# Triangular doubling in the recurrent stage: 32 of 64 columns per product, packed in PSUM, copied back with a stride

## The chip, the core and the metric

The kernel runs on one core of a Trainium2 chip. The metric is the device time of one execution in microseconds; the kernel before takes 2091.57 us (median of 3 runs, 2091.12 to 2100.21).

## What is computed

Two transformer blocks on one sequence of 512 tokens and width 1024. The change is in the second block, in its RWKV-7 branch (8 heads of 64, two directions). The reference computes it token by token:

```python
def step(state, inp):
    r_t, w_t, k_t, v_t, a_t, b_t = inp
    sa = jnp.einsum('dbhij,dbhj->dbhi', state, a_t)
    state = (state * w_t[..., None, :] + sa[..., :, None] * b_t[..., None, :]
             + v_t[..., :, None] * k_t[..., None, :])
    y = jnp.einsum('dbhij,dbhj->dbhi', state, r_t)
    return state, y
```

The kernel computes it in chunks of 64 tokens. Inside a chunk it needs the inverse of a triangular 64x64 matrix (identity minus the masked product of a and b). It gets it by doubling: the inverses of the 1x1 diagonal blocks give those of the 2x2 blocks, these those of the 4x4 blocks, and so on in six levels.

## The kernel before

`rwkv_block` holds the whole branch. Its engines run written-out programs in order, with semaphores between them, inside one block; the next stage (`merge_block`) starts its first weight load only when all engines have left it.

The work is cut into 8 units, `u`: four pairs of heads (`fi`) times two directions (`d = u % 2`). For one unit TensorE does in this order: `attention(u)`, the products of the scaled r, k, a, b (`r_bank<-r_b_s,r_a_s` and the like); the doubling levels `double(u, k)` for k = 1 to 5; between level 1 and 2 the products `keys_values(u)` and the two `lora_products` of the next unit; after level 5 `late(u)`: the product of the inverse with `wr`, the transposes of the next unit's tiles (`turn`), and the products that make the chunk's output and state. Level 0 is done on VectorE with masks (L2307).

At a level the tiles are `ab_t` (the masked matrix), `x` and `x_t` (the inverse so far and its transpose) and `z`. Each is 128 partitions by 2 heads (`hh`) by 4 token tiles (`NB`) by 64 columns; the lower and the upper 64 partitions are two chunks (`half`). A call of `block_products` (L2021) is one group: 8 matmuls of 64x64 weights, 4 tiles times 2 halves, each half on its own quadrant of the array. A matmul in f32 shows as two instructions in the trace, each with its own weight load. In a level TensorE does:

- two groups `ab_t` times `x`, one for each hh, into banks 4 and 5 (printed as `r_bank<-r_x,r_ab_t`: moving operand first, weights second);
- ScalarE copies each to `z` (L2227);
- then for each hh a group with `x_t` as weights and `z` moving (for `x`; not at level 5), and one with `z` as weights and `x_t` moving (for `x_t`);
- VectorE takes each result into `x` or `x_t` with `copy_predicated` under the level's mask (L2368, L2370), so that only the entries that the level changes are overwritten.

A unit has 28 such groups (10, 16 and 2 at level 5). The next level's first group waits for hh 0's copy into `x_t` and for the read of `z`. On VectorE the work of the next unit (`sums`, `directed`, `scale`, `unit_keys`) is written between the levels' copies, and on ScalarE its `rates` (two sigmoids behind a table load) and `decays` (three exponentials behind another).

Of the kernel before, what the change touches and what calls it, by code (L numbers as in the profile page):

```python
# [18 lines left out]
ACT = mybir.ActivationFunctionType  # L19
X = mybir.AxisListType.X  # L20

P = 128
# [15 lines left out]
CH = 64  # L38
# [5 lines left out]
NB = GRID // P  # L44
# [1833 lines left out]
def rwkv_block(nc, io, C, PV, zr, rw_t):  # L1878
# [6 lines left out]
    with ExitStack() as ctx:  # L1885
        def sem(name):
            return nc.alloc_semaphore(f"r_{name}")

        def sb(name, shape, dt=F32):
            return ctx.enter_context(nc.sbuf_tensor(f"r_{name}", shape, dt))  # L1890

        def column(name, k=0):
# [6 lines left out]
        levels = sb("levels", [P, 2, LEVELS, CH], U8)  # L1899
# [14 lines left out]
        ab_t, rb_t, ak_t, rk_t = (sb(n, [P, 2, NB, CH]) for n in ("ab_t", "rb_t", "ak_t", "rk_t"))  # L1914
        x, x_t, z = (sb(n, [P, 2, NB, CH]) for n in ("x", "x_t", "z"))
        wu = sb("wu", [P, 2, NB, 2, HD])
        gi = sb("gi", [P, NCH, NU, HD])
        s = sb("s", [P, NCH, NU, HD])
        pc = sb("pc", [P, NCH, NU])
        stat = reset[:, 0:16 * NB].rearrange("p (a b c) -> p a b c", a=2, b=NB)  # L1920
        bank = ctx.enter_context(nc.psum_tensor("r_bank", [P, 8, 512], F32))
# [1 line left out]
        in_loaded, reset_done, tanh_done, sqk, ksum, kstd, kmax, krec, kk_done, ka1_done, gate_sig = (  # L1923
            sem(n) for n in ("in_loaded", "reset_done", "tanh_done", "sqk", "ksum", "kstd", "kmax", "krec", "kk_done",
                             "ka1_done", "gate_sig"))
        levels_loaded, levels_done, masks_loaded, gate_loaded = (
            sem(n) for n in ("levels_loaded", "levels_done", "masks_loaded", "gate_loaded"))
        side_done, side_read, summed, c_done, e_done, kd1, kd_done, tt_done, bonus_done = (
            sem(n) for n in ("side_done", "side_read", "summed", "c_done", "e_done", "kd1", "kd_done", "tt_done", "bonus_done"))
        a_done, a_read, x_init, z_done, z_read, pr_done, cp_done = (  # L1930
            sem(n) for n in ("a_done", "a_read", "x_init", "z_done", "z_read", "pr_done", "cp_done"))
# [9 lines left out]
        tiles64 = lambda a: a.rearrange("p (a b) -> p a b", a=NB)  # L1941
        mask = lambda name: masks[:, CHUNK_MASKS.index(name), :]
        four = lambda m: m.unsqueeze(1).broadcast_to([P, NB, CH])
# [3 lines left out]
        two = lambda b, at: bank[:, b:b + 2, at:at + W].rearrange("p h (t f) -> p h t f", t=NB)  # L1947
        chunked = lambda a: a.rearrange("p (c n) -> p c n", c=NCH)
        hp = lambda hh: slice(64 * hh, 64 * hh + 64)
        level = lambda side, k: four(levels[:, side, k, :])  # L1950
        R_, K_, V_ = 0, RW_FI, 2 * RW_FI
        SIDE, PR = 7, 18
        W = NB * CH
        NZ = 2 * (LEVELS - 1)

        def pr_at(u, k, hh, of_t):

            return PR * u + (4 * (k - 1) + 2 * hh + of_t + 1 if k < LEVELS - 1 else 16 + hh + 1)
# [14 lines left out]
        def _(pe):  # L1973
# [43 lines left out]
            def block_products(out, left, right):  # L2017

                for t in range(NB):
                    for half in range(2):  # L2020
                        last = nc.tensor.matmul(out(half, t), left(half, t), right(half, t), start=True, stop=True)  # L2021
                return last

            def double(u, k):

                for hh in range(2):
                    if k == 1:
                        pe.wait_ge(a_read, 5 * u + 2)
                    else:
                        pe.wait_ge(cp_done, pr_at(u, k - 1, hh, 1))  # L2030
                        pe.wait_ge(z_read, NZ * u + 2 * (k - 2) + hh + 1)
                    block_products(lambda half, t: bank[hp(half), 4 + hh, t * CH:t * CH + CH],
                                   lambda half, t: ab_t[hp(half), hh, t, :], lambda half, t: x[hp(half), hh, t, :]).then_inc(z_done, 1)
                for hh in range(2):
                    pe.wait_ge(z_read, NZ * u + 2 * (k - 1) + hh + 1)
                    if k < LEVELS - 1:
                        if k == 1:
                            pe.wait_ge(a_read, 5 * u + 3)
                        block_products(lambda half, t: bank[hp(half), 2 + hh, t * CH:t * CH + CH],
                                       lambda half, t: x_t[hp(half), hh, t, :], lambda half, t: z[hp(half), hh, t, :]).then_inc(pr_done, 1)  # L2040
                    if k == 1:
                        pe.wait_ge(a_read, 5 * (u + 1))
                    block_products(lambda half, t: bank[hp(half), hh, t * CH:t * CH + CH],
                                   lambda half, t: z[hp(half), hh, t, :], lambda half, t: x_t[hp(half), hh, t, :]).then_inc(pr_done, 1)

            def keys_values(u):

# [60 lines left out]
            for u in range(NU):  # L2108
                attention(u)
                for k in range(1, LEVELS):  # L2110
                    double(u, k)
                    if k == 1:
                        keys_values(u)
                        if u + 1 < NU:
                            lora_products(u + 1)
                late(u)
# [42 lines left out]
        def _(act):  # L2159
            def rates(u):  # L2160

                fi, d = unit(u)
                if u:
                    act.wait_ge(tt_done, 4 * u)
                act.wait_ge(side_done, SIDE * u + 1)
                nc.scalar.activation(sg[:], bank[:, 6 + SIDE * u % 2, :], ACT.Sigmoid, bias=column("w0", 4 * d + fi)).then_inc(side_read, 1)
                act.wait_ge(side_done, SIDE * u + 2)
                nc.scalar.activation(rate[:], bank[:, 7 - SIDE * u % 2, :], ACT.Sigmoid, bias=column("a0", 4 * d + fi)).then_inc(side_read, 1)

            def decays(u):  # L2170
                act.wait_ge(c_done, u + 1)
                nc.scalar.activation(e_neg[:], cum[:], ACT.Exp, scale=KAPPA).then_inc(e_done, 1)
                nc.scalar.activation(e_pos[:], cum[:], ACT.Exp, scale=-KAPPA).then_inc(e_done, 1)
                nc.scalar.activation(before[:], before[:], ACT.Exp, scale=-KAPPA).then_inc(e_done, 1)
# [13 lines left out]
            def keys_values(u):  # L2188
                n = SIDE * u + 6
                act.wait_ge(side_done, n + 1)  # L2190
                nc.scalar.activation(wr[:, u % 2, :, :, HD:P], bank[:, 6 + n % 2, :].rearrange("p (h t f) -> p h t f", h=2, t=NB),
                                     ACT.Copy).then_inc(side_read, 1)
# [24 lines left out]
            for u in range(NU):  # L2217
                if u:
                    act.wait_ge(wu_done, 2 * u)
                else:  # L2220
                    act.wait_ge(masks_loaded, 16)
                for dst in (x_t, x):
                    nc.scalar.activation(blocks(dst[:]), eight(mask("ident")), ACT.Copy).then_inc(x_init, 1)
                for k in range(1, LEVELS):
                    for hh in range(2):
                        act.wait_ge(z_done, NZ * u + 2 * (k - 1) + hh + 1)
                        nc.scalar.activation(z[:, hh].rearrange("p a b -> p (a b)"), bank[:, 4 + hh, 0:W], ACT.Copy).then_inc(z_read, 1)  # L2227
                    if k == 1:
                        keys_values(u)
                    if u + 1 < NU:  # L2230
                        if k == 1:
                            rates(u + 1)
                        elif k == 3:
                            decays(u + 1)
                late(u)
# [15 lines left out]
        def _(dve):  # L2251
# [70 lines left out]
            def late(u):  # L2322
# [12 lines left out]
                else:  # L2335
                    dve.wait_ge(y0_read, u)
                    nc.vector.tensor_tensor(zr[:, V_ + fi, :], bank[:, 4, :], zr[:, V_ + fi, :], ALU.add).then_inc(y0_read, 1)

            nc.vector.memset(reset[:], 1.0).then_inc(reset_done, 1)
            nc.vector.memset(cum[:], 0.0).then_inc(reset_done, 1)  # L2340
            dve.wait_ge(reset_done, 2)
# [20 lines left out]
            for u in range(NU):  # L2362
                attention(u)
                for k in range(1, LEVELS):
                    for hh in range(2):
                        if k < LEVELS - 1:
                            dve.wait_ge(pr_done, pr_at(u, k, hh, 0))
                            nc.vector.copy_predicated(x[:, hh], level(u % 2, k), tiles64(bank[:, 2 + hh, 0:W])).then_inc(cp_done, 1)  # L2368
                        dve.wait_ge(pr_done, pr_at(u, k, hh, 1))
                        nc.vector.copy_predicated(x_t[:, hh], level(1 - u % 2, k), tiles64(bank[:, hh, 0:W])).then_inc(cp_done, 1)  # L2370
                    if u + 1 < NU:
                        if k == 1 and u % 2:
                            unit_keys(u // 2 + 1)
                        elif k == 2:
                            sums(u + 1)
                        elif k == 3:
                            directed(u + 1)
                        elif k == 4:
                            scale(u + 1)
                late(u)  # L2380
# [430 lines left out]
```

## Time and profile before

| | |
|---|---|
| median of 3 runs | 2091.57 us (2091.12 to 2100.21) |
| the profiled execution's own time | 2093.16 us |
| its span, first to last instruction | 2091.4 us |
| mean granted TensorE clock | 0.936 |
| TensorE busy | 1807.6 us (86%) |
| VectorE busy | 1025.6 us (49%) |
| ScalarE busy | 729.7 us (35%) |

The granted clock is a share of 2.4 GHz: 1.00 is 2.4 GHz and 0.50 is 1.2 GHz. PE rows are matmuls, PEld rows the weight loads that go with them. The recurrent stage takes from 1202 to 1544.6 us of the span.

### The profile page before, as it was taken

What the parts mean: (1) busy time and instruction counts of PE and PEld (TensorE: products, weight loads), DVE (VectorE), ACT (ScalarE), POOL (GpSimd) and SP (SyncE); (2) the same over time, 40 slices, a digit from 0 to 9 for tenths busy, and PEclk for the clock granted to TensorE, in tenths of its full rate; (3) what the DMA queues carried; (4) which work ended last, traced back from release to release, by engine and by line L of the source; (5) the groups of instructions that cost most, each with busy time, mean ns of one, the idle gap of its engine ahead of it and who ended that gap; (6) DMA issues with size and microseconds to landing.
All of it is one profiled execution on the core that took longest, in us unless ns stands there. A gap on an engine that the chain in (4) does not pass through costs nothing. (4 is left out here: it accounts for less than half of the span.)

```text
span 2091.4 us, 37559 instructions
## 1 busy us (share of the span) xinstructions
PE 1807.6 (86%) x16504; PEld 1542.5 (74%) x16504; DVE 1025.6 (49%) x1500; ACT 729.7 (35%) x1193; POOL 112.9 (5%) x133
## 2 busy tenths in 40 slices
PE   6999889838999999639999868888859899999988
PEld 5898768838989989438677657777738688878867
DVE  4145554456534635536454256756565544343445
ACT  3332234414434424223333253434233332232322
POOL 6000000030000000300000000000000200000020
PEclk9999979868999999769999989999979899999999
DMA  5211120102222222022122000000042122222221
GB/s 156 87 55 45 63 81 1 42 17 105 100 87 96 83 98 90 12 96 81 63 89 94 38 23 4 3 4 3 8 171 99 63 101 82 100 101 97 85 81 61
DMA packets 29256, 144.49 MB, mean 69 GB/s; under 512 B 6315, under 2 KB 9659, under 8 KB 14508
## 3 DMA queue, kind: packets, MB, share of 16 engines
q1 hardware_dynamic: 25116, 134.10, 17.9%
q0 software_dynamic: 3696, 7.35, 1.2%
q8 instruction: 126, 2.06, 0.4%
q10 hardware_dynamic: 288, 0.73, 0.1%
q14 instruction: 30, 0.25, 0.0%
HBM read 134.82 MB, written 8.91 MB: 69 GB/s over the span
## 5 line engine op out<-in xcount | busy, mean ns | idle before, releaser
L240 PE MATMUL f_bank<-f_u_hi,f_w_hi 128*128 128x258 f32 x704 | 201.1, 286 | 18.7 <-DVE f_w_lo L228 17.0
L241 PE MATMUL f_bank<-f_u_hi,f_w_lo 128*128 128x258 f32 x704 | 200.7, 285 | 0.0
L242 PE MATMUL f_bank<-f_u_lo,f_w_hi 128*128 128x258 f32 x704 | 199.1, 283 | 0.0
L240 PE MATMUL g_bank<-g_u_hi,g_w_hi 128*128 128x512 f32 x384 | 152.9, 398 | 17.0 <-DVE g_u_lo L2624 13.6
L241 PE MATMUL g_bank<-g_u_hi,g_w_lo 128*128 128x512 f32 x384 | 151.4, 394 | 0.0
L242 PE MATMUL g_bank<-g_u_lo,g_w_hi 128*128 128x512 f32 x384 | 151.2, 394 | 0.0
L240 PE MATMUL g_bank<-g_y_hi,g_w_hi 128*128 128x512 f32 x336 | 133.1, 396 | 18.5 <-DVE g_w_lo L228 11.7
L240 PEld LDWEIGHTS f_bank<-f_u_hi,f_w_hi 128*128 128x128 f32 x704 | 133.4, 190 | 20.3 <-DVE f_w_lo L228 17.8
L215 ACT ACTIVATE g_w_hi<-g_w_raw 128x2048 fp32r<-128x2048 f32 x45 | 85.9, 1909 | 174.4 <-PE g_bank L242 172.0
L242 PEld LDWEIGHTS f_bank<-f_u_lo,f_w_hi 128*128 128x128 f32 x704 | 134.4, 191 | 0.0
L241 PEld LDWEIGHTS f_bank<-f_u_hi,f_w_lo 128*128 128x128 f32 x704 | 133.8, 190 | 0.0
L241 PE MATMUL g_bank<-g_y_hi,g_w_lo 128*128 128x512 f32 x336 | 132.5, 394 | 0.0
L242 PE MATMUL g_bank<-g_y_lo,g_w_hi 128*128 128x512 f32 x336 | 132.3, 394 | 0.0
L228 DVE TENSOR_TENSOR g_w_lo<-g_w_raw,g_w_hi 128x2048 fp32r<-128x2048 f32 x45 | 103.2, 2292 | 48.5 <-ACT g_w_hi L215 48.3
L240 PEld LDWEIGHTS g_bank<-g_u_hi,g_w_hi 128*128 128x128 f32 x384 | 73.0, 190 | 39.5 <-issue 20.0
L228 DVE TENSOR_TENSOR f_w_lo<-f_w_raw,f_w_hi 128x2048 fp32r<-128x2048 f32 x34 | 77.9, 2292 | 47.8 <-ACT f_w_hi L215 47.7
L1606 PE MATMUL a_bank<-a_u_hi,a_w_hi 128*128 128x512 f32 x240 | 98.6, 411 | 1.3 <-ACT a_qkv L1705 0.6
L1610 PE MATMUL a_bank<-a_u_lo,a_w_hi 128*128 128x512 f32 x240 | 98.3, 409 | 0.0
L1608 PE MATMUL a_bank<-a_u_hi,a_w_lo 128*128 128x512 f32 x240 | 98.0, 408 | 0.0
L240 PEld LDWEIGHTS g_bank<-g_y_hi,g_w_hi 128*128 128x128 f32 x336 | 64.1, 191 | 34.6 <-issue 17.0
L242 PEld LDWEIGHTS g_bank<-g_u_lo,g_w_hi 128*128 128x128 f32 x384 | 73.3, 191 | 15.7
L2634 DVE TENSOR_TENSOR h<-g_bank,h 128x512 f32<-128x512 f32 x40 | 27.7, 691 | 114.8 <-PE g_bank L242 114.8
(445 smaller groups left out, 4319.1 us busy)
## 6 DMA issues: line engine op xcount, KB each, us to landing
g_w_raw<-in_w_ff SPq DMA_DIRECT2D x32, 1024.0 KB, 4.8
f_w_raw<-in_w_ffn_in SPq DMA_DIRECT2D x22, 1024.0 KB, 4.8
a_w_raw<-in_w_in SPq DMA_DIRECT2D x18, 1024.0 KB, 4.9
m_w_raw<-in_w_in SPq DMA_DIRECT2D x12, 1024.0 KB, 4.8
f_w_raw<-in_w_ffn_out SPq DMA_DIRECT2D x12, 1024.0 KB, 4.8
m_w_raw<-in_w_o SPq DMA_DIRECT2D x4, 1024.0 KB, 5.1
gate_pre<-rw_t POOLq DMA_DIRECT2D x16, 256.0 KB, 2.3
g_w_raw<-in_w_up SPq DMA_DIRECT2D x4, 1024.0 KB, 8.8
```

The source lines that it names most:

```text
L215: nc.scalar.activation(R.hi[:, r, 0:size], R.raw[:, r, 0:size], ACT.Copy).then_inc(R.hi_done, 1)
L228: nc.vector.tensor_tensor(R.lo[:, r, 0:size], R.raw[:, r, 0:size], R.hi[:, r, 0:size].bitcast(F32), ALU.subtract).then_inc(R.split, 1)
L240: nc.tensor.matmul(out, w_hi, u_hi, start=start, stop=False)
L241: nc.tensor.matmul(out, w_lo, u_hi, start=False, stop=False)
L242: return nc.tensor.matmul(out, w_hi, u_lo, start=False, stop=stop)
L1606: nc.tensor.matmul(tile_bank(g), w_hi, u_hi[:, k, :], start=k == 0, stop=False)
L1608: nc.tensor.matmul(tile_bank(g), w_lo, u_hi[:, k, :], start=False, stop=False)
L1610: last = nc.tensor.matmul(tile_bank(g), w_hi, u_lo[:, k, :], start=False, stop=k == KT - 1)
L2634: nc.vector.tensor_tensor(x[:, t, :], bank[:, (2 * r + m) % 4, :], x[:, t, :], ALU.add).then_inc(R.tile_free, 1)
```

## The change

The masks of level k change only every other run of 2^k columns: in `x` the even runs for direction 0 and the odd ones for direction 1, in `x_t` the other way round. The changed kernel streams only these 32 of the 64 columns as the moving operand of every doubling product. The weights stay whole (64 columns). The 32 result columns lie packed in PSUM (128 in place of 256 elements per partition for one hh); ScalarE writes them into their places in `z`, and VectorE into those of `x` and `x_t`, with a stride. `z` is cleared once by VectorE at the start of the stage, since half of its columns are not written at first. `keys_values` and `late` use the same helper with 64 and 128 columns as before.

```diff
+        HALF_W = NB * CH // 2
+        parity = lambda a, k, par: a.rearrange("p (n s b) -> p n s b", s=2, b=1 << k)[:, :, par, :]
+        parities = lambda a, k, par: a.rearrange("p t (n s b) -> p t n s b", s=2, b=1 << k)[:, :, :, par, :]
+        packed = lambda b, k: bank[:, b, 0:HALF_W].rearrange("p (t n b) -> p t n b", t=NB, b=1 << k)
...
             def double(u, k):
 
+                d = u % 2
+                compact = lambda b: lambda half, t: bank[hp(half), b, t * CH // 2:t * CH // 2 + CH // 2]
                 for hh in range(2):
                     if k == 1:
                         pe.wait_ge(a_read, 5 * u + 2)
+                        pe.wait_ge(z_clear, 1)
                     else:
                         pe.wait_ge(cp_done, pr_at(u, k - 1, hh, 1))
                         pe.wait_ge(z_read, NZ * u + 2 * (k - 2) + hh + 1)
-                    block_products(lambda half, t: bank[hp(half), 4 + hh, t * CH:t * CH + CH],
-                                   lambda half, t: ab_t[hp(half), hh, t, :], lambda half, t: x[hp(half), hh, t, :]).then_inc(z_done, 1)
+                    block_products(compact(4 + hh), lambda half, t: ab_t[hp(half), hh, t, :],
+                                   lambda half, t: parity(x[hp(half), hh, t, :], k, d)).then_inc(z_done, 1)
...
-                        block_products(lambda half, t: bank[hp(half), 2 + hh, t * CH:t * CH + CH],
-                                       lambda half, t: x_t[hp(half), hh, t, :], lambda half, t: z[hp(half), hh, t, :]).then_inc(pr_done, 1)
+                        block_products(compact(2 + hh), lambda half, t: x_t[hp(half), hh, t, :],
+                                       lambda half, t: parity(z[hp(half), hh, t, :], k, d)).then_inc(pr_done, 1)
...
-                        nc.scalar.activation(z[:, hh].rearrange("p a b -> p (a b)"), bank[:, 4 + hh, 0:W], ACT.Copy).then_inc(z_read, 1)
+                        nc.scalar.activation(parities(z[:, hh], k, u % 2), packed(4 + hh, k), ACT.Copy).then_inc(z_read, 1)
...
+            nc.vector.memset(z[:], 0.0).then_inc(z_clear, 1)
             nc.vector.memset(reset[:], 1.0).then_inc(reset_done, 1)
...
-                        nc.vector.copy_predicated(x_t[:, hh], level(1 - u % 2, k), tiles64(bank[:, hh, 0:W])).then_inc(cp_done, 1)
+                        nc.vector.copy_predicated(parities(x_t[:, hh], k, 1 - u % 2), level(1 - u % 2, k), packed(hh, k)).then_inc(cp_done, 1)
```

TensorE's order at levels 1 and 2 of unit 0, before (shapes are weight rows x moving columns):

```order
L2021 MATMUL r_bank<-r_x,r_ab_t 64x64 x16
L2021 MATMUL r_bank<-r_z,r_x_t 64x64 x8
L2021 MATMUL r_bank<-r_x_t,r_z 64x64 x8
L2021 MATMUL r_bank<-r_v_tm,r_ak_t 64x64 x16
L1982 MATMUL r_bank<-zr,r_lora 128x512
```

The same place in the changed kernel, where `block_products` is L2028:

```order
L2028 MATMUL r_bank<-r_x,r_ab_t 64x32 x16
L2028 MATMUL r_bank<-r_z,r_x_t 64x32 x8
L2028 MATMUL r_bank<-r_x_t,r_z 64x32 x8
L2028 MATMUL r_bank<-r_v_tm,r_ak_t 64x64 x16
L1989 MATMUL r_bank<-zr,r_lora 128x512
```

No instruction is added, removed or moved on TensorE: the number of matmuls, and so of weight loads, is the same, and only the moving columns of the doubling are halved.

ScalarE's order from unit 0's first copy to `z` on, before:

```order
L2227 ACTIVATE r_z<-r_bank 128x256 x2
L2191 ACTIVATE r_wr<-r_bank 128x8x64
L2166 ACT_TABLE_LOAD
L2166 ACTIVATE r_sg<-r_bank,params 128x512
L2168 ACTIVATE r_rate<-r_bank,params 128x512
L2227 ACTIVATE r_z<-r_bank 128x256 x4
```

And in the changed kernel:

```order
L2237 ACTIVATE r_z<-r_bank 128x64x2 x2
L2201 ACTIVATE r_wr<-r_bank 128x8x64
L2176 ACT_TABLE_LOAD
L2176 ACTIVATE r_sg<-r_bank,params 128x512
L2178 ACTIVATE r_rate<-r_bank,params 128x512
L2237 ACTIVATE r_z<-r_bank 128x32x4 x2
L2237 ACTIVATE r_z<-r_bank 128x16x8 x2
```

The copies stand where they stood and carry 128 elements per partition in runs of 2, 4, 8, 16 and 32 elements at levels 1 to 5.

## Rows read from the trace of the kernel before

**Rows 1.** Windows: length; busy us (instructions) of PE, PEld, DVE, ACT, POOL; clock; DMA

```profile
1226.00:1501.00 275.00, 233.87 (x6977) 203.50 (x6967) 168.53 (x309) 109.11 (x205) 0.00 (x0) 0.99 0.02 4
```

**Rows 2.** Timeline, first weight load of the next stage

```profile
1544.71 0.33 SPq L2479 DMA_DIRECT2D g_w_raw<-in_w_up  x1
```

**Rows 3.** Timeline of VectorE, where the first and the last unit begin

```profile
1227.33 0.69 DVE L2304 TENSOR_TENSOR r_ab_t<-r_bank,r_masks 128x512 f32<-128x512 f32 x1 [5.27 <-ACT r_x L2223]
...
1476.53 0.69 DVE L2304 TENSOR_TENSOR r_ab_t<-r_bank,r_masks 128x512 f32<-128x512 f32 x1 [1.98 <-ACT r_x L2223]
```

**Rows 4.** Timeline of unit 2 from level 2 to the transposes: start, duration, engine

```profile
1308.36 0.66 ACT L2227 ACTIVATE r_z<-r_bank 128x256 f32<-128x256 f32 x2
...
1309.78 0.63 PE L2021 MATMUL r_bank<-r_z,r_x_t 64*64 64x64 f32 x16
...
1310.25 0.63 PE L2021 MATMUL r_bank<-r_x_t,r_z 64*64 64x64 f32 x16
...
1318.42 0.75 DVE L2284 SCALAR_TENSOR_TENSOR r_bz<-r_kdir,params,zr 128x512 f32<-128x512 f32 x1
...
1321.57 0.77 DVE L2370 COPY_PREDICATED r_x_t<-r_levels,r_bank 128x256 f32<-128x256 uint8 x2
...
1322.15 1.96 PE L2021 MATMUL r_bank<-r_wr,r_x_t 64*64 64x128 f32 x32 [1.72 <-DVE r_x_t L2370]
...
1324.04 0.66 PE L1991 MATMUL r_bank<-consts,r_a_s 128*128 128x128 f32 x4
```

**Rows 5.** Groups by form: copies and doubling products, mean ns of one

```profile
L2021 PE MATMUL r_bank<-r_x_t,r_z 64*64 64x64 f32 x1280 | 52.0, 219 | 0.4 <-issue 0.2
L2370 DVE COPY_PREDICATED r_x_t<-r_levels,r_bank 128x256 f32<-128x256 uint8 x80 | 34.5, 441 | 3.9 <-PE r_bank L2021 2.8
L2227 ACT ACTIVATE r_z<-r_bank 128x256 f32<-128x256 f32 x80 | 29.4, 382 | 70.8 <-PE r_bank L2021 70.0
...
L2307 DVE COPY_PREDICATED r_x_t<-r_levels,r_bank 128x512 f32<-128x512 uint8 x8 | 5.7, 714 | 0.0
...
L1741 ACT ACTIVATE a_k_t<-a_bank 128x128 f32<-128x128 f32 x4 | 1.1, 286 | 0.0
```

**Rows 6.** Timeline, f32 matmuls with 128-column weights and 16 moving columns

```profile
197.86 1.03 PE L657 MATMUL m_bank<-consts,m_vg 16*128 16x16 f32 x8
```

**Rows 7.** Weight loads by form: full clock (two), half clock (two)

```profile
L660 PEld LDWEIGHTS m_bank<-m_vg,consts 16*16 16x16 f32 x4 | 0.3, 91 | 0.3
...
L2021 PEld LDWEIGHTS r_bank<-r_wr,r_x_t 64*64 64x64 f32 x32 | 1.8, 133 | 1.8 <-issue 1.8
...
L835 PEld LDWEIGHTS m_bank<-m_vg,m_pm 16*16 16x16 f32 x16 | 1.6, 140 | 0.2 <-issue 0.2
...
L2021 PEld LDWEIGHTS r_bank<-r_wr,r_x_t 64*64 64x64 f32 x22 | 2.4, 226 | 0.0
```

**Rows 8.** Timeline of unit 3, the `wr` product mostly at half clock

```profile
1357.84 3.30 PE L2021 MATMUL r_bank<-r_wr,r_x_t 64*64 64x128 f32 x32 [1.72 <-DVE r_x_t L2370]
...
1361.08 0.93 PE L1991 MATMUL r_bank<-consts,r_a_s 128*128 128x128 f32 x4
```

**Rows 9.** Windows view of six stretches (columns as in rows 1)

```profile
1307.07:1310.49 3.42, 2.29 (x80) 2.15 (x76) 0.92 (x3) 1.94 (x5) 0.00 (x0) 1.00 0.02 5
...
1313.90:1317.31 3.41, 2.71 (x82) 2.44 (x80) 3.38 (x10) 2.32 (x5) 0.00 (x0) 1.00 0.02 5
...
1354.86:1358.27 3.41, 1.68 (x44) 1.43 (x42) 3.17 (x8) 0.38 (x1) 0.00 (x0) 1.00 0.02 5
1358.27:1361.69 3.42, 3.42 (x32) 3.09 (x28) 0.00 (x0) 1.10 (x2) 0.00 (x0) 0.50 0.00 0
...
197.80:201.20 3.40, 3.34 (x23) 2.38 (x22) 0.85 (x3) 0.99 (x4) 0.00 (x0) 0.99 0.00 0
201.20:204.50 3.30, 2.24 (x10) 2.27 (x11) 1.69 (x9) 2.71 (x5) 0.00 (x0) 0.50 0.02 5
```

**Rows 10.** Timeline of VectorE, its first work after the stage's memsets

```profile
1210.01 0.43 DVE L2350 TENSOR_SCALAR rw_t<-rw_t 128x512 f32<-128x512 f32 x1 [6.33 <-ACT rw_t L2212]
```

More of the change, by code:

```diff
@@ L1925, in rwkv_block @@
                              "ka1_done", "gate_sig"))
-        levels_loaded, levels_done, masks_loaded, gate_loaded = (
-            sem(n) for n in ("levels_loaded", "levels_done", "masks_loaded", "gate_loaded"))
+        levels_loaded, levels_done, masks_loaded, gate_loaded, z_clear = (
+            sem(n) for n in ("levels_loaded", "levels_done", "masks_loaded", "gate_loaded", "z_clear"))
         side_done, side_read, summed, c_done, e_done, kd1, kd_done, tt_done, bonus_done = (
@@ L1949, in rwkv_block, with level @@
         hp = lambda hh: slice(64 * hh, 64 * hh + 64)
-        level = lambda side, k: four(levels[:, side, k, :])
+        HALF_W = NB * CH // 2
+        parity = lambda a, k, par: a.rearrange("p (n s b) -> p n s b", s=2, b=1 << k)[:, :, par, :]
+        parities = lambda a, k, par: a.rearrange("p t (n s b) -> p t n s b", s=2, b=1 << k)[:, :, :, par, :]
+        packed = lambda b, k: bank[:, b, 0:HALF_W].rearrange("p (t n b) -> p t n b", t=NB, b=1 << k)
+        def level(side, k):
+            return parity(levels[:, side, k, :], k, side).unsqueeze(1).broadcast_to([P, NB, CH >> (k + 1), 1 << k])
         R_, K_, V_ = 0, RW_FI, 2 * RW_FI
@@ L2038, in double @@
                             pe.wait_ge(a_read, 5 * u + 3)
-                        block_products(lambda half, t: bank[hp(half), 2 + hh, t * CH:t * CH + CH],
-                                       lambda half, t: x_t[hp(half), hh, t, :], lambda half, t: z[hp(half), hh, t, :]).then_inc(pr_done, 1)
+                        block_products(compact(2 + hh), lambda half, t: x_t[hp(half), hh, t, :],
+                                       lambda half, t: parity(z[hp(half), hh, t, :], k, d)).then_inc(pr_done, 1)
                     if k == 1:
                         pe.wait_ge(a_read, 5 * (u + 1))
-                    block_products(lambda half, t: bank[hp(half), hh, t * CH:t * CH + CH],
-                                   lambda half, t: z[hp(half), hh, t, :], lambda half, t: x_t[hp(half), hh, t, :]).then_inc(pr_done, 1)
+                    block_products(compact(hh), lambda half, t: z[hp(half), hh, t, :],
+                                   lambda half, t: parity(x_t[hp(half), hh, t, :], k, 1 - d)).then_inc(pr_done, 1)
             def keys_values(u):
@@ L2367, in _ @@
                             dve.wait_ge(pr_done, pr_at(u, k, hh, 0))
-                            nc.vector.copy_predicated(x[:, hh], level(u % 2, k), tiles64(bank[:, 2 + hh, 0:W])).then_inc(cp_done, 1)
+                            nc.vector.copy_predicated(parities(x[:, hh], k, u % 2), level(u % 2, k), packed(2 + hh, k)).then_inc(cp_done, 1)
                         dve.wait_ge(pr_done, pr_at(u, k, hh, 1))
-                        nc.vector.copy_predicated(x_t[:, hh], level(1 - u % 2, k), tiles64(bank[:, hh, 0:W])).then_inc(cp_done, 1)
+                        nc.vector.copy_predicated(parities(x_t[:, hh], k, 1 - u % 2), level(1 - u % 2, k), packed(hh, k)).then_inc(cp_done, 1)
                     if u + 1 < NU:
```

## The prediction

> **What bounds the kernel now.** I read the windows by stage first, then the timeline of one unit, then the groups by form. The eight units take 1226 to 1501, and TensorE is busy 233.87 of these 275 us, VectorE 168.53, ScalarE 109.11 [rows 1]. The next stage's first weight load starts at 1544.71, after every engine has left the stage [rows 2], so what the units save or lose the span saves or loses. Seven unit periods lie between the first and the last start, 249.2 us, 35.6 us each [rows 3].
>
> In a unit the timeline shows a chain that changes engines. At level 2 ScalarE's sigmoids release `z` at 1308.36; then TensorE runs group after group, one every 0.47 us (1309.78, 1310.25). Later VectorE is the last: its `scale` work of the next unit begins at 1318.42, its two copies into `x_t` follow at 1321.57, and only then, at 1322.15, can the `wr` product start [rows 4]. From 1308.8 to 1322.15 there are 22 groups, 10.3 us of 13.3: TensorE is the larger part, the copies and VectorE's queue the rest.
>
> **What a group of 32 columns costs.** A group is 16 instructions on two quadrants, so 8 rounds of 0.058 us. Two things go on in a round: 64 columns stream, and the next 64 weight columns load. The question is which of the two sets 0.058. In f32 matmuls with 128 weight columns and only 16 moving ones at full clock, eight take 1.03 us with a last one of some 0.26, so one every 0.11 us [rows 6]. Sixteen columns can't take this long to stream; the load does. A load of 16 columns takes 91 ns and one of 64 columns 133 ns [rows 7]: 42 ns for 48 columns, 0.88 ns per column, 56 ns for 64. That is the whole round. So I cost the halved stream at nothing: a group stays at 0.47 us. The other end, if loads didn't count, is half, 0.24 us.
>
> The Trainium skill says the same of loads in "TensorE: Matmul & The Clock Gate", LDWEIGHTS (loading the stationary operand): the time is the number of weight columns over 1.2 GHz, 53 ns for 64. By that rule the change saves no TensorE time at full clock, and the rows agree.
>
> **What the copies save.** ScalarE's copy to `z` takes 382 ns for 256 elements, and a copy of 128 from PSUM 286: 0.10 us less. VectorE's `copy_predicated` takes 714 ns for 512 and 441 for 256, so about 305 for 128: 0.14 us less [rows 5]. In unit 2 the `z` copy at level 2 is on the path once (0.10). One copy stands between the levels' groups at level 3 (0.14). VectorE's queue before `sums` and `scale` sheds some more, about 0.3 over eight copies, since most of them wait for TensorE's 0.47 us anyway, and the last copy before `wr` 0.14. That makes 0.7 us per unit. Runs of 2 elements with a stride I take at the price of a plain copy; the bound above is the present price, and the saving is gone. The memset of `z` and its wait cost nothing: VectorE idles 6.33 us for ScalarE just behind its first memsets [rows 10], and level 1 is 20 us away. Without this cover it would be half a microsecond, once.
>
> At an unchanged clock the sum is 7 x 0.7 and about 0.7 for the last unit: 5.6 us less.
>
> **What the clock does.** In these units the granted clock is 0.99 [rows 1], 2.4 GHz, but it isn't safe. In the stretch 1354.86 to 1358.27, the end of level 5 and VectorE's `scale`, TensorE had 44 instructions of 64 or 128 columns, and then the clock fell to 0.50, 1.2 GHz; the `wr` product and the next transposes in that half-clock stretch are followed by full clock again. TensorE's busy time alone doesn't hold it: from 197.80 on the engine was busy 3.34 of 3.40 us, with the narrow matmuls of [rows 6] among its 23, and the clock fell all the same [rows 9]. The change leaves the instructions in place and takes half of what each streams. Around level 2's wait for the sigmoids (1307.07) a stretch has 80 instructions, at levels 3 and 4 (1313.90) 82 [rows 9]; with 32 columns they stream what 40 and 41 do now, fewer than the 44 before that fall. So I expect the clock to fall in each unit that has the next unit's work between its levels (0 to 6), at about the turn from level 2 to 3, and to stay down: slower rounds stream still less in the same time. It comes back when 64- and 128-column products run densely, in `late`.
>
> At 1.2 GHz the loads slow down too: 140 ns for 16 columns and 226 for 64 [rows 7], 86 ns for 48, 1.8 ns per column, 115 ns for 64. A round is then 0.115 and a group 0.92 us. In unit 2, if the fall comes at 1310.1, three groups of level 2's products are done; 1 + 6 + 6 + 4 = 17 groups remain. 17 x 0.92 = 15.6, and about 0.7 for the last drain and copies (VectorE's and ScalarE's own work now fits into the longer levels, so the 0.7 saved above is swallowed). `wr` starts at 1326.4 in place of 1322.15: 4.25 more. The `wr` product mostly at half clock took from 1357.84 to 1361.08, 3.24 us [rows 8], against 1.89 at full clock [rows 4]: 1.35 more. I add an estimated 0.4 for transposes behind it. That is 6.0 us per unit, 42 for seven. The last unit has no other work between its levels and runs its groups back to back; I count no change there. **2091.6 + 42 gives 2133 us.** The profiled execution's own time is 2093.16 for a span of 2091.4, within the runs' spread, so I add to the median.
>
> The Trainium skill's advice in the same page, "HAM oscillation", speaks only of idle gaps of TensorE as what brings the clock down. The gaps stay or shrink here, so by it the clock would hold and the sum would be 2086. The fall at 201.20, behind a nearly gapless stretch, speaks against it.
>
> **Bounds of the clock's part.** If the clock comes back ahead of `wr`, or falls half a level later, a unit loses about 3.5: 2091.6 + 25 = 2116. If it falls at level 1, `keys_values`' two groups (2 x 0.45) and five more groups of level 2 (5 x 0.45) run at half clock too: 9.2 per unit, 64 for seven, and with a last unit of which 18 groups fall as well (8 us) 2163.
>
> **Rivals.**
> - *The clock falls* (forecast, all variants): 0.68; likeliest 2133, its own 8-in-10 range 2112 to 2160.
> - *The clock holds, loads bind*: only the copies gain, 2086. For it: the trace has only two falls in these rows, neither with streams of 32 columns, and what a narrow stream counts for is read from one stretch of mixed matmuls. 0.20. It is the result on the other side: not slower. It decides if the narrower streams don't count for less than wide ones.
> - *The stream binds and the clock holds*: a group takes 0.24 us. VectorE's copies at 0.31 then set the pace; a level's four products end 0.6 sooner, and with the `ab_t` group and copies a unit loses about 3 us: 2068. The 0.11 us of [rows 6] speak against it. 0.05.
> - *Strided copies cost more than plain ones* at full clock, say 0.45 us for each of 20 on the path per unit in place of 0.3: 3 per unit, 2115. Nothing in the rows speaks for it. 0.07, whatever the clock.
>
> Within 0.5% (2081 to 2102, about what a measurement can tell from no change) lies the second: 0.20. Faster: 0.06. Slower: 0.74. The range reaches down to the second rival: 2084 to 2160.
>
> **What the profile after would show.** The granted clock over the units well below 0.99, near 0.75, with half-clock stretches that begin at levels 2 and 3 of each unit and end in `late`; PEld of the doubling with a mean of 170 to 200 ns in place of 134. The same number of matmul and load instructions. Groups at 0.47 us where the clock is full, whatever their columns. Copies near 290 and 305 ns. The prediction is wrong if the clock stays at 0.99; its size is wrong if half-clock groups take other than 0.92, or the clock returns elsewhere.

## The result, and the profile after the change

The changed kernel takes 2135.49 us (median of 4 runs, 2128.08 to 2144.09), the kernel before 2095.49 us on the same chip (4 runs, 2091.12 to 2100.21). The ratio is 1.019, 95% interval 1.014 to 1.024: slower by 40 us. The profiled execution is the shortest of the four, 2128.08 us for a span of 2126.3, 34.9 us over the span before.

First the page of the changed kernel, TensorE's busy row and the granted clock in 40 slices:

```profile
PE 1856.8 (87%) x16504; PEld 1596.3 (75%) x16504; DVE 1013.0 (48%) x1501; ACT 724.5 (34%) x1193; POOL 112.8 (5%) x133
...
PEclk8999979869999999679999877687879899999999
```

The instructions are the same in number. The clock is lower in the slices from about 1220 to 1540 us, in which units 0 to 6 and the start of the last lie. The view by windows of the same kernel (columns as in [rows 1]) gives first the seven unit periods, then three stretches around unit 2, then the last unit up to the next stage. Below it stand the same two spans of the kernel before:

```profile
1228.18:1513.93 285.75, 262.79 (x6232) 238.24 (x6231) 144.75 (x284) 96.53 (x189) 0.00 (x0) 0.75 0.02 4
...
1300.16:1320.64 20.48, 17.64 (x589) 15.22 (x587) 8.15 (x16) 7.99 (x16) 0.00 (x0) 1.00 0.02 4
1320.64:1341.12 20.48, 20.07 (x312) 19.34 (x309) 10.60 (x24) 6.64 (x14) 0.00 (x0) 0.50 0.01 2
1341.12:1361.60 20.48, 17.56 (x556) 14.04 (x554) 12.66 (x18) 7.28 (x14) 0.00 (x0) 1.00 0.01 3
...
1513.93:1580.08 66.15, 43.51 (x1220) 37.55 (x1208) 41.93 (x90) 12.25 (x24) 0.00 (x0) 0.90 0.01 2
```

```profile
1227.33:1476.53 249.20, 210.77 (x6172) 181.69 (x6166) 155.45 (x283) 102.29 (x189) 0.00 (x0) 0.99 0.02 4
...
1476.53:1544.71 68.18, 44.76 (x1231) 38.26 (x1223) 44.12 (x90) 13.25 (x24) 0.00 (x0) 0.87 0.01 3
```

The unit starts are where VectorE writes `r_ab_t`; the tile view groups its eight, and the timeline has the next stage's first weight load:

```profile
L2314 DVE TENSOR_TENSOR r_ab_t<-r_bank,r_masks x8: 691/692/692, 1228.2 to 1513.9; 128x512 f32<-128x512 f32 x8
```

```profile
1580.08 0.80 SPq L2490 DMA_DIRECT2D g_w_raw<-in_w_up  x2
```

Against [rows 2, 3] the first unit starts 0.85 us later, a unit period is 285.75 / 7 = 40.8 us instead of 35.6, and the last unit takes 66.15 us instead of 68.18. 0.85 + 7 x 5.22 - 2.03 = 35.4 us, which is how much later the weight load comes. So the whole loss lies in the seven unit periods. In the half-clock stretch TensorE is busy 20.07 of 20.48 us, with 312 instructions; in the full-clock stretches beside it it is idle almost 3 us and does 556 and 589.

The groups by form, with the answers to [rows 5]:

```profile
L2028 PE MATMUL r_bank<-r_x_t,r_z 64*64 64x32 f32 x1280 | 71.2, 264 | 1.4 <-issue 1.2
L2028 PEld LDWEIGHTS r_bank<-r_x_t,r_z 64*64 64x64 f32 x1280 | 65.0, 189 | 2.6 <-issue 1.8 <-DVE r_ak_t L2314 0.2
...
L2381 DVE COPY_PREDICATED r_x_t<-r_levels,r_bank 128x128 f32<-128x128 uint8 x80 | 25.2, 323 | 26.7 <-PE r_bank L2028 26.6
...
L2237 ACT ACTIVATE r_z<-r_bank 128x128 f32<-128x128 f32 x80 | 21.6, 281 | 103.7 <-PE r_bank L2028 103.6
```

A product streams 32 columns instead of 64 and takes longer, 264 ns on average instead of 219. The copies got cheaper, and ScalarE and VectorE wait for TensorE more. The timeline of unit 2 (it began at 1308.31) shows where: two groups at full clock, three at half, then `wr`, the first transposes and the first product behind them; and VectorE's copies at levels 1 and 2:

```profile
1312.24 0.44 DVE L2379 COPY_PREDICATED r_x<-r_levels,r_bank 128x128 f32<-128x128 uint8 x1 [0.16 <-PE r_bank L2028]
...
1319.44 0.63 PE L2028 MATMUL r_bank<-r_x_t,r_z 64*64 64x32 f32 x16
...
1319.91 0.63 PE L2028 MATMUL r_bank<-r_z,r_x_t 64*64 64x32 f32 x16
1320.13 0.30 DVE L2381 COPY_PREDICATED r_x_t<-r_levels,r_bank 128x128 f32<-128x128 uint8 x1 [0.17 <-PE r_bank L2028]
...
1323.58 1.05 PE L2028 MATMUL r_bank<-r_x_t,r_z 64*64 64x32 f32 x16
...
1324.44 1.05 PE L2028 MATMUL r_bank<-r_z,r_x_t 64*64 64x32 f32 x16
...
1325.29 1.05 PE L2028 MATMUL r_bank<-r_x_t,r_z 64*64 64x32 f32 x16
...
1335.29 3.68 PE L2028 MATMUL r_bank<-r_wr,r_x_t 64*64 64x128 f32 x32 [0.41 <-DVE r_x_t L2381]
...
1338.90 1.11 PE L1998 MATMUL r_bank<-consts,r_a_s 128*128 128x128 f32 x4
...
1343.46 0.69 PE L2079 MATMUL r_bank<-r_rb_t,r_wu 64*64 64x64 f32 x32
```

A group still starts every 0.47 us at full clock, and every 0.85 us at half. The clock falls at 1320.64, at the turn from level 2 to 3, and returns at 1341.12, among the transposes. In the kernel before, unit 2 began at 1297.51, and the first product behind its transposes at 1327.85; level 2's first two groups ran at 1306.52, ahead of the wait for ScalarE:

```profile
1297.51 0.69 DVE L2304 TENSOR_TENSOR r_ab_t<-r_bank,r_masks 128x512 f32<-128x512 f32 x1 [2.43 <-ACT r_x L2223]
...
1306.52 1.15 PE L2021 MATMUL r_bank<-r_x,r_ab_t 64*64 64x64 f32 x32
...
1327.85 0.69 PE L2069 MATMUL r_bank<-r_rb_t,r_wu 64*64 64x64 f32 x32
```

### The profile page after: what moved, and what is told of

It is laid out like the page before. It is cut to its first block and busy times, and to the rows that moved or that the text cites. A ratio compares the mean times of both kernels' runs of the same rounds, so it can differ in the third digit from the quotient of the medians.

```text
span 2126.3 us, 37576 instructions
## 1 busy us (share of the span) xinstructions
PE 1856.8 (87%) x16504; PEld 1596.3 (75%) x16504; DVE 1013.0 (48%) x1501; ACT 724.5 (34%) x1193; POOL 112.8 (5%) x133
## 5 line engine op out<-in xcount | busy, mean ns | idle before, releaser
L240 PEld LDWEIGHTS g_bank<-g_y_hi,g_w_hi 128*128 128x128 f32 x336 | 64.0, 190 | 34.6 <-issue 17.0
L241 PEld LDWEIGHTS g_bank<-g_u_hi,g_w_lo 128*128 128x128 f32 x384 | 73.1, 190 | 14.3
```

The costliest lines, as they stand in the source:

```text
L240: nc.tensor.matmul(out, w_hi, u_hi, start=start, stop=False)
L241: nc.tensor.matmul(out, w_lo, u_hi, start=False, stop=False)
```

## Experiments

Theory: the narrow stream, and nothing else in the change, brings the clock down in units 0 to 6; at full clock it saves nothing, and the copies save a little. Rivals: the copies or the packing cost the time; the clock falls for another reason (idle gaps). The experiments ran on several chips, each beside the kernel before on the same chip, so kernels are compared by their ratios to it.

### The two halves of the change apart

Wide products, half-width copies: `block_products` gets all 64 columns again, and the copies pick their 32 from the full width of PSUM.

```diff
-block_products(compact(4 + hh), ab_t..., parity(x[hp(half), hh, t, :], k, d))
+block_products(wide(4 + hh), ab_t..., x[hp(half), hh, t, :])       # the other two likewise
-nc.scalar.activation(parities(z[:, hh], k, u % 2), packed(4 + hh, k), ACT.Copy)
+nc.scalar.activation(parities(z[:, hh], k, u % 2), picked(4 + hh, k, u % 2), ACT.Copy)
```

> This kernel undoes the narrow stream alone: every product of the levels again streams all 64 columns and writes the full width of PSUM, and ACT's and DVE's copies still take only the 32 columns that the level changes, read and written with a stride. Theory (the narrow stream is what brings the granted clock down; the copies by themselves save time): the groups of 8 products stay at 0.47 us, the clock in the units goes back to 0.93 to 1.0, and the unit takes what it took before (35.6 us) less 0 to 0.7 us, so the time is 0 to 6 us under the kernel before. Rival A (the strided copies are what made the unit longer): the unit stays well above 35.6 us, and the time stays 20 us or more above the kernel before. Rival B (the stream of 64 columns had been what bound the group, and the narrow one gained time that something else took away): groups of products here are longer than the 0.46 to 0.47 us seen in the full-clock stretches of the changed kernel.

> As the kernel with wide products and half-width copies, but at level 1, where the changed columns lie in runs of 2, the three copies take all 64 columns as before the change. In the trace of the changed kernel DVE's predicated copy took 439 to 440 ns at level 1 and 296 at level 2. Theory (a short run, not the stride, costs there): level 1's copies cost 441 ns on DVE and 380 on ACT, the others 296 to 305 and 281, and the time is the same as the other kernel's within 2 us, as the DVE copy costs the same either way and ACT's is about 0.1 us dearer once or twice a unit. Rival (level 1's copy is dear for another reason, for instance contention with PE at that place): it stays 440 here too but so it would full-width, so the durations at level 1 in the half-copy kernel decide: 440 there as well with wide products says that it is the run of 2.

> The other half of the change alone: products stream only the 32 columns that the level changes, but write them spread, each to its own place in the full width of PSUM, and ACT's and DVE's copies take all 64 columns as before the change. Theory (the narrow stream alone brings the clock down): the granted clock in the units is 0.74 to 0.80 as in the changed kernel, the unit takes 40.5 to 42 us, a group of products 0.47 us at full clock and 0.85 at half, and the time is 30 to 50 us over the kernel before. Rival A (the packing or the strided copies cause the loss): the time is near the kernel before, within 6 us. Rival B (spread writes into PSUM are slower than packed ones): the group at full clock is over 0.50 us, and the time exceeds the changed kernel's by more than the copies' 0.7 us a unit, 6 us in all.

Measured, against 2093.66 us for the kernel before in these rounds: wide products with half-width copies 2085.65 us, ratio 0.996 (0.995 to 0.998); with level 1's copies at full width 2084.27, ratio 0.996 (0.995 to 0.997); narrow products with full-width copies 2143.10, ratio 1.024 (1.021 to 1.026). The windows of the seven unit periods, first with wide products and half-width copies, then the reverse:

```profile
1227.62:1469.80 242.18, 205.65 (x6184) 179.04 (x6176) 142.94 (x283) 94.57 (x189) 0.00 (x0) 1.00 0.02 5
```

```profile
1225.29:1515.50 290.21, 263.35 (x6171) 237.95 (x6164) 159.22 (x283) 103.76 (x189) 0.00 (x0) 0.75 0.02 4
1515.50:1594.09 78.59, 55.36 (x1230) 49.41 (x1222) 44.09 (x90) 13.38 (x25) 0.00 (x0) 0.74 0.01 2
```

The halves have opposite signs. With wide products the period is 34.6 us at clock 1.00; with narrow ones 41.5 us at 0.75, close to the 40.8 at 0.75 of the changed kernel. The strided copies are a gain (the 8.0 us are more than the 0 to 6 that I had expected), and the packing isn't to blame. Idle time isn't either: with wide products TensorE idles more, 36.5 of 242.18 us against 23.0 of 285.75 in the changed kernel, and keeps its full clock. What no run separates is the number of columns from the way they are read: every narrow product of levels 1 to 4 also reads its moving operand in short runs with a stride, and no kernel here streams 32 columns in one piece at those levels. In the narrow kernel the last unit falls too: 78.59 us at 0.74, against 66.15 at 0.90 in the changed kernel.

The copies' own rows, from the timeline of the kernel with wide products, at level 1 and level 2:

```profile
1300.82 0.44 DVE L2379 COPY_PREDICATED r_x<-r_levels,r_bank 128x128 f32<-128x128 uint8 x1 [0.22 <-PE r_bank L2028]
...
1308.50 0.30 DVE L2379 COPY_PREDICATED r_x<-r_levels,r_bank 128x128 f32<-128x128 uint8 x1 [5.09 <-PE r_bank L2028]
```

Where the changed columns lie in runs of 2, VectorE's copy of half the elements costs what the full one costs, 0.44 us; from runs of 4 on it costs 0.30. This holds with wide and narrow products. The mask is read in the same runs as `x` is written, so which of the two makes short runs dear isn't shown. Whether level 1's copies are half or full makes no difference that the whole time shows (2085.65 and 2084.27 us).

### Streaming given back as work that nothing needs

```diff
+def filler(count):
+    for _ in range(count):
+        for half in range(2):
+            nc.tensor.matmul(bank[hp(half), 4, W:2 * W], ab_t[hp(half), 0, 0, :],
+                             ab_t[hp(half), 0].rearrange("p t f -> p (t f)"), start=True, stop=True)
...
+                    if u + 1 < NU and hh == 0:
+                        filler((0, 0, 2, 1, 1, 1)[k])      # ahead of level k's first product
...
+                if u + 1 < NU:
+                    filler(3)                              # ahead of wr's product
```

> The changed kernel with work added that nothing reads: pairs of matmuls that stream 256 columns under 64-column weights into an unused part of a PSUM bank, in every unit but the last 2 pairs ahead of level 2's first product group, 1 pair ahead of each of levels 3, 4 and 5, and 3 pairs ahead of the product for wr, 8 pairs a unit. At full clock a pair of 2 x 256 columns in two halves of the array adds 0.2 to 0.45 us, so 8 pairs add up to 3.4 us a unit where PE is the only thing waited for. Theory (the clock falls because PE streams too few columns while busy, not because of the engine's idle time): the granted clock in units 0 to 6 rises from 0.75 to 0.78 towards 0.9 or more, and the unit takes 36 to 39 us against the changed kernel's 40.8, so the time falls by 10 to 30 us against the changed kernel in spite of the added work; it does not reach the kernel before unless the pairs lie in PE's waits. Rival (idle gaps between the groups, or something unrelated to the stream, bring the clock down): the clock stays at 0.75 to 0.8 and the time is over the changed kernel's by up to 24 us.

> The changed kernel with only the last of the added work: 3 pairs of matmuls that stream 256 columns ahead of the product for wr, once in each of units 0 to 6, and none among the levels. In the changed kernel the half-clock stretches begin and end among the levels as well as near wr, about 20.5 us each. Theory (what counts is how much PE streams in the stretch itself): added columns only at the end of a unit leave the levels as thin as they were, so half-clock stretches stay, fewer or shorter than without: the time is 2105 to 2145 us, over that of the kernel with all 8 pairs. Rival (a fall begins in the gap before wr and then lasts through the next levels): covering that gap is enough, and the time is 2085 to 2100 us.

With all 8 pairs: 2108.96 us (four runs, 2088.55 to 2114.82), ratio to before 1.008 (1.005 to 1.011). With the last 3 pairs alone: 2136.89, ratio 1.020 (1.017 to 1.022). The first kernel's windows over the seven periods, and groups by form:

```profile
1224.68:1472.80 248.12, 231.36 (x6401) 195.74 (x6394) 143.52 (x283) 95.56 (x189) 0.00 (x0) 0.97 0.02 5
```

```profile
L2028 PE MATMUL r_bank<-r_x_t,r_z 64*64 64x32 f32 x1258 | 50.3, 221 | 1.0 <-issue 1.0
...
L2035 PE MATMUL r_bank<-r_ab_t 64*64 64x256 f32 x224 | 32.5, 400 | 0.2
```

224 more matmul instructions (112 matmuls), busy 32.5 us, and the kernel is 26 us faster than the changed one by the medians (ratio 1.008 against 1.019); the profiled execution by 40 us, with one short fall and a period of 35.4 us. The narrow products are back at 221 ns. A kernel that becomes faster by added work has a clock problem: this is the strongest of the runs. Its four runs spread over 26 us, and its profile is the fastest of them. The last 3 pairs alone give nothing back: 1.020 against the changed kernel's 1.019, and in the profile a period of 43.1 us at clock 0.74. So covering the gap before `wr` isn't enough. Whether it is the place or the smaller amount (3 pairs instead of 8) isn't shown. The windows of that kernel show two half-clock stretches in which TensorE has no idle time at all:

```profile
1327.90:1348.38 20.48, 20.48 (x337) 19.36 (x336) 11.24 (x26) 4.62 (x10) 0.00 (x0) 0.50 0.01 2
...
1372.27:1389.34 17.07, 17.07 (x270) 15.91 (x270) 9.39 (x21) 4.62 (x10) 0.00 (x0) 0.50 0.01 2
```

So idle gaps aren't what keeps it down (ends of matmuls are modelled in a trace, but the weight loads too are busy 19.36 and 15.91 us). The Trainium skill ("TensorE: Matmul & The Clock Gate", HAM oscillation) explains oscillation by waits between bursts of matmuls; these rows don't agree.

### How many products must be narrow, and which

Against the kernel with wide products and half-width copies:

```diff
-block_products(wide(4 + hh), ab_t..., x[hp(half), hh, t, :])
+block_products(compact(4 + hh), ab_t..., parity(x[hp(half), hh, t, :], k, d))   # the first product alone
```

> The kernel with wide products and half-width copies, but the first of a level's three products (ab_t by x) streams only the 32 changed columns, packed; the other two stream 64. So 1280 of 3584 level products are narrow instead of all or none. Theory (the clock falls by how little PE streams): the granted clock in the units and the time lie between those of the two kernels that differ only in this, 2086 us with no narrow product and 2135 us with all, at 2095 to 2125 us, with half-clock stretches in some of the units. Rival (a fall needs something only the fully narrow kernel has, such as the narrow write of x): the time stays within 3 us of 2086 us. Rival B (one narrow product already sets off the alternation of half and full clock): 2130 us or more.

> The changed kernel, but the first of a level's products (ab_t by x) streams all 64 columns; the two others, 2304 of 3584 level products, stream the 32 changed ones. With the kernels that differ only in this, it makes a series: none narrow 2086 us, 1280 of 3584 narrow 2098 us, all narrow 2135 us. Theory (how far the clock falls goes with how little is streamed in all): half-clock stretches longer than the single short ones seen with one narrow product, the time at 2105 to 2132 us. Rival (the first product, which stands alone between waits, is the one that matters): under 2100 us. Rival B (two narrow products are enough for the full alternation): 2132 to 2140 us.

> The changed kernel, but the last of a level's products (z by x_t, 1280 of 3584) streams all 64 columns; the first (ab_t by x) and the second (x_t by z), 2304 of 3584, stream the 32 changed ones. As many products are narrow as in the kernel whose first product is wide (2091.8 us), but now the first is among them, as in the kernel in which it alone is narrow (2097.8 us). Theory A (only the number of narrow products counts): 2089 to 2095 us, the same as with the first product wide. Theory B (the first product counts for more, since it stands between two waits, where PE streams least): 2098 to 2125 us, and more half-clock time in the units than in the trace of the kernel with the first product wide (granted clock 0.95 over the seven unit periods).

| narrow products | of 3584 instructions | us | ratio to before | clock, seven periods |
|---|---|---|---|---|
| none | 0 | 2085.65 | 0.996 (0.995 to 0.998) | 1.00 |
| first | 1280 | 2097.84 | 1.001 (1.000 to 1.003) | 0.97 |
| second, third | 2304 | 2091.84 | 0.999 (0.997 to 1.001) | 0.95 |
| first, second | 2304 | 2111.74 | 1.010 (1.008 to 1.012) | 0.85 |
| all | 3584 | 2135.49 | 1.019 (1.014 to 1.024) | 0.75 |

The rows of the two kernels with 2304 narrow products, by windows, that with the first product wide and that with the third wide:

```profile
1225.80:1475.10 249.30, 215.07 (x6210) 189.43 (x6206) 143.73 (x284) 95.33 (x190) 0.00 (x0) 0.95 0.02 4
```

```profile
1226.98:1496.70 269.72, 237.93 (x6183) 213.60 (x6177) 144.16 (x283) 95.42 (x189) 0.00 (x0) 0.85 0.02 4
```

My expectation for the second and third (2105 to 2132) failed: the number of narrow products doesn't decide by itself. With the number held at 2304, the intervals lie apart (0.997 to 1.001 and 1.008 to 1.012), so the first product counts for more than the third, as I had expected of the last of these kernels (2098 to 2125). That this is because it stands between two waits is argued, not shown. The clock doesn't fall in proportion either. The partly narrow kernels mostly have shorter falls; with the first and second narrow, three of the seven units still stay at half clock for 14 to 17 us, until shortly before `wr`, and only in the fully narrow kernel all seven do so, and through `wr`.

### The last unit alone

```diff
+narrow = u == NU - 1
+n = CH // 2 if narrow else CH
+wide = lambda b: lambda half, t: bank[hp(half), b, t * n:t * n + n]
+cols = lambda v, par: parity(v, k, par) if narrow else v
```

> The kernel with wide products and half-width copies in units 0 to 6, and the whole change (32 packed columns) in the last unit alone. Theory: in the last unit the levels run at full clock with narrow products too, a group of 8 products takes 0.47 us either way, and the time is within 3 us of 2086 us. Rival (the narrow stream gains where the clock holds, and the last unit's 2.0 us gain in the changed kernel came from it): 2 us or more under the kernel with wide products everywhere. Rival B (the narrow stream brings the clock down in the last unit as well, since it no longer follows a stretch at half clock): the last unit is 4 us or more longer.

2087.59 us, ratio 0.999 (0.997 to 1.001), 2 us over wide products everywhere (0.996). The profiled last unit takes 66.74 us against 67.64, clock 0.90 against 0.87. But the twelve runs fall into seven of 2083.2 to 2089.0 and five of 2094.1 to 2102.1, a spread that wide products (2083.25 to 2089.53) don't have. The mean granted clock is 0.935 to 0.939 in the seven and 0.928 to 0.932 in the five. A fall in the last unit in those five, as in the trace of narrow products with full-width copies, would account for it, but the only profile is of one of the seven. The first rival, a gain in the time, is out.

### What a round is made of

```diff
-block_products(wide(4 + hh), lambda half, t: ab_t[hp(half), hh, t, :],
+block_products(wide(4 + hh), lambda half, t: ab_t[hp(half), hh, t, 0:CH // 2],    # the others likewise
...
+nc.vector.memset(levels[:, :, 1:LEVELS, :], 0)
```

> A measurement of what binds a group of products at full clock. All level products stream 64 columns as before, but the weights loaded for them are 32 columns instead of 64, so half of the output rows are not computed, and the masks of levels 1 to 5 are zero, so that x and x_t keep what they had: the inverse is not computed, the rest of the work is as in the kernel with wide products and half-width copies. Theory (the weight load of 64 columns fills the round of 0.058 us per matmul; 32 or 64 moving columns fit beside it): 8 matmuls take 0.23 to 0.35 us instead of 0.47, and the unit gets shorter by 4 to 12 us from 34.6, where the clock holds. Rival (a fixed time per matmul or its issue binds): 8 matmuls stay at 0.46 to 0.47 us, and the time stays within 5 us of 2086 us. If the clock falls in this kernel the groups of its full-clock stretches decide.

> Halves both sides of a round at once: the level products stream the 32 packed columns as in the changed kernel, and load 32 columns of weights as in the kernel with half weights. Half of the output rows are not computed and the masks of levels 1 to 5 are zero, so the inverse is not computed. Known so far: two matmuls, one on each half of the array, start every 58.3 ns with 64 weight columns, whether 64 or 32 columns stream, and every 55.7 ns with 32 weight columns and 64 streamed ones. Theory (a round is the longer of the load and the stream, and both are near 56 ns for 64 columns): in full-clock stretches the round falls to 27 to 40 ns, a group of 16 products to 0.22 to 0.32 us instead of 0.47. Rival (a fixed 55 to 58 ns per pair whatever the columns): 55 ns or more here too. Of the clock: with so little streamed it is at half for as much of the units as in the changed kernel or more, so the whole time is 2100 to 2150 us, and only the rounds at full clock decide.

A group is 8 matmuls, which are 16 instructions in the trace, two to a round; "a group of 16 products" means these instructions. Half weights: 2085.06 us, ratio 0.996. Half weights and half stream: 2083.73 us (2079.26 to 2092.01), ratio 0.995 (0.993 to 0.996). Timelines of weight loads, first with 64 streamed columns, at full clock, then with 32, at half clock (1274.50) and at full (from 1280.82):

```profile
1236.48 0.51 PEld L2028 LDWEIGHTS r_bank<-r_x_t,r_z 64*32 64x32 f32 x16
1236.92 0.50 PEld L2028 LDWEIGHTS r_bank<-r_z,r_x_t 64*32 64x32 f32 x16
```

```profile
1274.50 0.53 PEld L2028 LDWEIGHTS r_bank<-r_x_t,r_z 64*32 64x32 f32 x16
1274.93 0.53 PEld L2028 LDWEIGHTS r_bank<-r_z,r_x_t 64*32 64x32 f32 x16
...
1280.82 0.34 PEld L2028 LDWEIGHTS r_bank<-r_x_t,r_z 64*32 64x32 f32 x16
1281.08 0.34 PEld L2028 LDWEIGHTS r_bank<-r_z,r_x_t 64*32 64x32 f32 x16
1281.33 0.34 PEld L2028 LDWEIGHTS r_bank<-r_x_t,r_z 64*32 64x32 f32 x16
```

Halving the load alone gives groups every 0.44 to 0.45 us, not the 0.23 to 0.35 that I had expected. Halving the stream alone gives 0.47. Halving both gives 0.25 us at full clock (the last three rows) and 0.43 at half (the first two of the five). These times fit a round that is the longer of a load and a stream, which run beside each other; at 64 columns both fill it. A fixed time per matmul that would hold a round at 0.056 us is out. The Trainium skill says that TensorE reads weights and moving columns over two independent ports ("TensorE: Matmul & The Clock Gate", Step-by-step: what each phase is for); these rows agree in that the two go on together. The whole time missed the expectation of 2100 us or more. The profiled execution, the longest of six, has a clock of 0.86 over the seven periods and a period of 35.5 us against 34.6 with wide products, 0.9 more; the median isn't above that of wide products. With rounds half as long, the low clock costs little.

## Why the prediction was right, and where its sizes were off

- **A group stays at 0.47 us at full clock**: right (1319.44, 1319.91). The reason was half of the truth: the load fills the round, but the stream of 64 columns did too (0.44 us a group with half the load, 0.25 with half of both). For this change it makes no difference; for one that narrows the weights it would.
- **The clock falls at the turn from level 2 to 3 in units 0 to 6**: right. 1320.64 in unit 2, clock 0.75 over the seven periods. The runs add what was only read from [rows 9]: narrow products alone do it, added streaming undoes much of it, idle time doesn't explain it. The argument from columns per stretch was a guess from one fall; whether columns or the strided reading count, no run says.
- **17 groups of 0.92 us, `wr` 4.25 us later**: mis-sized. 16 groups at 0.85 us are 13.6 instead of 15.6 us, and `wr` starts 26.98 us after the unit's start instead of 24.64 (1322.15 less 1297.51), 2.3 us later. The slope of 1.8 ns per column from [rows 7] was too steep; a round at half clock is 0.107 us, not 0.115.
- **The `wr` product, 1.35 us more**: mis-sized, it took 3.61 us (1335.29 to 1338.90) instead of 1.89, 1.7 more, since all of it lies at half clock; in [rows 8] only most of it did.
- **Transposes, 0.4**: mis-sized, from the first to `late`'s first product 4.56 us instead of 3.81, 0.75 more.
- **The sum, 6.0 us per unit**: 5.2 on average. The three terms of unit 2 give 2.3 + 1.7 + 0.75 = 4.8 of its 5.1. Two terms were too small and one too large, 36.5 us for seven instead of 42. In the other executions the loss is larger: by the medians it is 40.0 us for the whole kernel. And the base was 3.9 us low (2091.57, where four runs give 2095.49). So that 2133 and 2135.5 lie so close is in part luck: the errors cancel.
- **22 groups from 1308.8 to 1322.15**: there are 20, 9.4 us of 13.3, since level 2's first two run at 1306.52. The sum doesn't use it.
- **The last unit unchanged**: 2.0 us less in the profile, of which the copies are some 0.5 (68.18 before, 67.64 with wide products and half-width copies); less half-clock time behind the levels (0.90 against 0.87) is probably most of the rest. To count no change there was too sure: in the trace of narrow products with full-width copies the last unit did fall and took 78.59 us, 10.4 more than before.
- **The copies save 0.7 us per unit**: about right in sum. Wide products with half-width copies have a period 1.0 us shorter, of which the two short falls of the kernel before (clock 0.99) are a part, and the median is 8.0 us lower where 5.6 was the sum. At level 1 VectorE's copy saves nothing: the bound named for runs of 2, the present price, was the value.
- **Rivals**: the clock that holds and the stream that binds fell with the first trace. Strided copies aren't dear: VectorE's cost no more than the full ones even in runs of 2.

Open stays what exactly of the stream counts in which place. The kernel to keep is the one with wide products and half-width copies: it beats both, by 0.4% and 2.2% by the ratios.

## What to carry to other kernels

Before narrowing what TensorE streams, ask which of load and stream fills a round: where both do, halving one saves nothing, and the engine may fall to half clock while it is busy all the time. Look at the granted clock, not at the busy share: 98% busy and half as many instructions per us is the sign. Take the part of such a change that saves work on the other engines (here the half-width copies) and leave the wide stream.

## What the runs showed of the hardware

- With streams of 32 columns under loads of 64, the clock was at 1.2 GHz while TensorE was busy 20.07 of 20.48 us, and even 20.48 of 20.48; with streams of 64 it stayed at 2.4 GHz (1.00 over the seven periods).
- VectorE's `copy_predicated` of 128 elements per partition: 0.44 us where they lie in runs of 2, 0.30 us from runs of 4 on; ScalarE's copy hardly differs (0.29 and 0.28).
- TensorE didn't mind reading runs of 2. With half the load and half the stream, level 1's groups at full clock also start every 0.25 us, as this timeline shows. Written spread over PSUM in runs of 2, in the kernel with narrow products and full-width copies, level 1's group starts every 0.46 us (the second timeline); but there the load fills the round, and a stream of 64 columns fits beside it as well, so a spread write of 32 that took up to twice as long would not show.

```profile
1232.74 0.34 PEld L2028 LDWEIGHTS r_bank<-r_z,r_x_t 64*32 64x32 f32 x16
1232.99 0.34 PEld L2028 LDWEIGHTS r_bank<-r_x_t,r_z 64*32 64x32 f32 x16
```

```profile
1356.93 0.54 PEld L2030 LDWEIGHTS r_bank<-r_x_t,r_z 64*64 64x64 f32 x16
1357.39 0.55 PEld L2030 LDWEIGHTS r_bank<-r_z,r_x_t 64*64 64x64 f32 x16
```
